# One decoder layer in float32: packed query, key and router products, routing by match-and-replace, and another order and grain of work and weight loads around the first experts

## What is computed

```
xn   = rms_norm(h, g);  proj = xn @ w_in          # columns: cq 384, ckv 256, kr 32, rx 1024, rg 1024, gates 2048
q    = rms_norm(cq) @ w_uq                        # 8 heads x (64 plain + 32 rotary)
kv   = rms_norm(ckv) @ w_ukv                      # 8 heads x (64 key + 64 value); rotary key kr is shared by the heads
attn = softmax(q k^T * scale, causal) @ v @ w_ao
rec  = RG-LRU(conv(rx), gates) * gelu(rg) @ w_ro
h    = h + (sigmoid(ga) * attn + sigmoid(gr) * rec) @ w_out
x2   = rms_norm(h);  logits = x2 @ w_router + b_router       # 32 experts
top 4 of 32, gates = softmax of the four logits
h    = h + sum over the chosen experts of gate * (swiglu(x2 @ w_up[e] + b_up[e]) @ w_down[e] + b_down[e])
out  = rms_norm(h)[16:]
```

## Time and profile before

| | |
|---|---|
| median of 3 executions | 1181.56 us (1181.07 to 1181.73) |
| the profiled execution | 1181.36 us |
| its span, first to last instruction | 1179.6 us |
| TensorE busy | 1141.4 us, 97% |
| VectorE, ScalarE busy | 228.5 us (19%), 187.3 us (16%) |
| chain that ended last | PE 73%, DMA 25%, ACT 1% |
| moved | 442.03 MB, mean 375 GB/s |
| TensorE clock granted | full in all 40 slices of the page, mean 0.999 |

### The profile page before, as it was taken

The page is one execution under the profiler, slowest core; times in us unless marked ns, Lnnn a source line. Parts: engine busy times, 40 slices in busy tenths (PEclk is TensorE's granted clock), DMA queues, the critical chain, the costliest instruction groups (busy, mean ns, idle before and its releaser), DMA issues.

```text
span 1179.6 us, 13314 instructions
## 1 busy us (share of the span) xinstructions
PE 1141.4 (97%) x5598; PEld 530.4 (45%) x5598; DVE 228.5 (19%) x528; ACT 187.3 (16%) x404; POOL 0.2 (0%) x4
## 2 busy tenths in 40 slices
PE   9999999999999999999999999999998989898997
PEld 7767888855243333333343433333333333333332
DVE  4555621114111111111111112111111111111112
ACT  2257620002011110101010111101000001010102
POOL 0000000000000000000000000000000000000000
PEclk9999999999999999999999999999999999999999
DMA  9834434387999999999999999999999999999996
GB/s 377 348 143 179 150 119 162 146 344 290 399 422 429 428 431 432 432 431 430 434 430 432 432 432 431 430 434 430 432 432 432 431 431 433 431 431 432 426 426 272
DMA packets 26128, 442.03 MB, mean 375 GB/s; under 512 B 4144, under 2 KB 4656, under 8 KB 7408
## 3 DMA queue, kind: packets, MB, share of 16 engines
q1 hardware_dynamic: 23472, 439.19, 88.3%
q10 hardware_dynamic: 2624, 2.39, 0.6%
HBM read 440.52 MB, written 1.05 MB: 374 GB/s over the span
## 4 chain that ended last, share of the span: by engine, by line
PE 73%; DMA 25%; ACT 1%; DVE 0%; issue 0%; SPq 0%; another core or an unknown queue 0%; ACTq 0%; DVEq 0%
PE ps L880 28%; DMA work<-in_w_exp_dram 24%; PE ps L899 12%; PE ps L538 11%; PE ps L867 4%; PE ps L855 4%; PE ps L747 2%; PE ps L810 2%; PE ps L830 2%; PE ps L771 1%; PE ps L615 1%; ACT work L1297 1%; PE ps L889 1%; DMA ring<-in_w_mix_dram 1%; PE ps L581 1%; PE ps L861 1%
## 5 line engine op out<-in xcount | busy, mean ns | idle before, releaser
L880 PE MATMUL ps<-ring,work 128*64 128x512 f32 x1536 | 341.0, 595 | 12.6 <-DMA ring<-in_w_exp_dram 12.6
L880 PEld LDWEIGHTS ps<-ring,work 128*64 128x64 f32 x1536 | 109.0, 137 | 228.9 <-issue 217.6
L1733 DVE TENSOR_SCALAR work<-ps 128x512 f32<-128x512 f32 x32 | 22.1, 691 | 742.2 <-PE ps L880 742.2
L538 PE MATMUL ps<-work,ring 128*128 128x256 f32 (+2 forms) x576 | 129.5, 384 | 0.0
L880 PE MATMUL ps<-work 128*64 128x512 f32 x512 | 116.2, 596 | 5.1 <-DMA work<-in_w_exp_dram 5.1
L899 PE MATMUL ps<-ring,work 128*64 128x512 f32 x512 | 113.6, 595 | 5.5 <-ACT work L1297 3.8
L899 PE MATMUL ps<-work 128*64 128x512 f32 x512 | 114.0, 596 | 3.9 <-ACT work L1297 3.8
L538 PEld LDWEIGHTS ps<-work,ring 128*128 128x128 f32 (+1 forms) x576 | 107.1, 188 | 19.1 <-issue 1.2
L880 PEld LDWEIGHTS ps<-work 128*64 128x64 f32 x512 | 34.9, 137 | 82.1 <-issue 72.6
L899 PEld LDWEIGHTS ps<-ring,work 128*64 128x64 f32 x512 | 35.5, 137 | 73.4 <-issue 65.4
L899 PEld LDWEIGHTS ps<-work 128*64 128x64 f32 x512 | 35.2, 137 | 72.8 <-issue 62.8
(11 more groups left out here) (237 smaller groups left out, 617.3 us busy)
## 6 DMA issues: line engine op xcount, KB each, us to landing
ring<-in_w_exp_dram SPq DMA_DIRECT2D x52, 4096.0 KB, 39.9
work<-in_w_exp_dram SPq DMA_DIRECT2D x26, 4096.0 KB, 39.9
ring<-in_w_exp_dram SPq DMA_DIRECT2D x23, 2048.0 KB, 10.8
ring<-in_w_mix_dram SPq DMA_DIRECT2D x29, 1024.0 KB, 7.1
work<-in_w_exp_dram SPq DMA_DIRECT2D x10, 2048.0 KB, 12.2
work<-in_w_exp_dram SPq DMA_DIRECT2D x4, 1024.0 KB, 44.4
...
```

Source lines behind the costliest of these rows:

```text
L538: ins = nc.tensor.matmul(ps[part:part + width, b, 0:hi - lo], wv[:, k, o:o + width], xnT[:, k, lo:hi], start=(k == 0), stop=(k == KT - 1))
L880: ins = nc.tensor.matmul(ps[CAP * c:CAP * c + CAP, b, :], xeT[:, k, CAP * (u % 2):CAP * (u % 2) + CAP], wu[:, k % SPAN, 512 * q:512 * q + ...
L1733: V.tensor_scalar(hg, ps[:, 0, :], LIMIT, None, ALU.min).then_inc(glu_ready, 1)
```

## The change

The 32-column product of the rotary key is done in four column groups, whose partial sums a second small product adds up (`fold`) beside the rotation. The query weights are repacked on the host so that six full tiles of 128 columns replace eight of 96: four with two heads' plain parts each, two with four heads' rotary parts; the query rotation is one set of four 32x32 matmuls in one bank, and VectorE's part works on 128 partitions. The router has its weights as stationary operand in four column groups and h^T moving; ScalarE copies the result and a small product turns and adds it (`fold(i)`). The mask comes from match-and-replace: the first four columns of `lgs` hold a large constant, so that MAX8 gives that and the top four, match-and-replace writes a constant over these, and a comparison with the logits gives `selm`, per tile (`choose`). Seeds, bias and router are put in another order; the norm of tile 1 is made in halves; of expert 0's gathers the second goes behind k = 1, the b_down product behind `up`; expert 1 has its own order with the scatters behind `up` and the gathers between the steps of `down`; `down` frees slot by slot. SP loads five units (`HALVED`) of experts 2 and 3 in halves and uses units of 2 MB until expert 7, pairs from expert 8 on. Constants for rotation, cos and sin are spread over all 128 partitions, which makes the constants 32 columns (16 KB) longer.

The diff, cut to its core and less indented (`...` marks what is left out):

```diff
+HALVED = (0, 4, 5, 10, 11)
...
-    spe.wait_ge(xn2_ready, TT)
+    spe.wait_ge(xn2_ready, TT + 1)
     fetch(1, 4)
...
+    for n in range(2, 8):
+        for c in range(UNITS_E):
+            r = UNITS_E * (n % 2) + c
+            used = M0 + PER_EXPERT * (n - 2) + SPAN * c
+            if n < 4 and r in HALVED:
+                for h in range(SPAN):
+                    spe.wait_ge(weights_used, used + h + 1)
+                    spe.dma_start(RING[r][:, SLOT * h:SLOT * h + SLOT],
+                                  w_exp[n, c // 2, :, UNIT * (c % 2) + SLOT * h:UNIT * (c % 2) + SLOT * h + SLOT])\
+                       .then_inc(unit_loaded[r], 16)
+            else:
+                spe.wait_ge(weights_used, used + SPAN)
+                fetch(n, c)
...
-        spe.dma_start(PAIR[3 * (u % 2) + p], w_exp[it * UNROLL + (u + 4), p, :, :])\
+        spe.dma_start(PAIR[3 * (u % 2) + p], w_exp[it * UNROLL + (u + 8), p, :, :])\
...
-    project(("kr", 0), OFF_KR, ROPE, 0, T, part=NOPE, last=True)
...
+    for k in range(KT):
+        q = ROPE * (k % 4)
+        ins = nc.tensor.matmul(ps[q:q + ROPE, b, 0:T], wv[:, k, o:o + ROPE], xnT[:, k, :], start=(k < 4), stop=(k >= 4))
+        if k == 0:
+            settle(ins)
+    ins.then_inc(proj_done, 1)
...
-    nc.tensor.matmul(ps[NOPE:QD, 6, 0:T], rotm, kh[NOPE:QD, 0, :], start=True, stop=True).then_inc(krot_done, 1)
+    nc.tensor.matmul(ps[NOPE:QD, 6, 0:T], rotm, krope, start=True, stop=True)
+    nc.tensor.matmul(ps[NOPE:QD, 7, 0:T], foldm, krope, start=True, stop=True).then_inc(krot_done, 1)
...
-    for h in range(HEADS):
-        n = load_at[("uq", 384 * (h // 4))]
+    for t in range(6):
...
-            ins = nc.tensor.matmul(ps[0:QD, b, 0:SEQ], wv[:, k, QD * (h % 4):QD * (h % 4) + QD], cq[:, k, :],
+            ins = nc.tensor.matmul(ps[:, b, 0:SEQ], wv[:, k, P * (t % 3):P * (t % 3) + P], cq[:, k, :],
...
-        if g >= 2:
-            if g == 2:
-                pe.wait_ge(proj_read, JOB[("q", HEADS - 1)] + 1)
-                pe.wait_ge(rope_ready, 1)
-                pe.wait_ge(lora_var, 2)
-            for r in (2 * g - 4, 2 * g - 3):
-                nc.tensor.matmul(ps[NOPE:QD, 4 + r, :].rearrange("p (h t) -> p h t", h=2), rotm,
-                                 qh[NOPE:QD, 2 * r:2 * r + 2, :], start=True, stop=True).then_inc(qrot_done, 1)
+        if g == 2:
+            pe.wait_ge(proj_read, JOB[("q", 5)] + 1)
+            pe.wait_ge(lora_var, 2)
+            for j in range(4):
+                ins = nc.tensor.matmul(ps[ROPE * j:ROPE * j + ROPE, 4, :].rearrange("p (k t) -> p k t", k=2),
+                                       rotm[ROPE * j:ROPE * j + ROPE, :], qrope[ROPE * j:ROPE * j + ROPE, :, :],
+                                       start=True, stop=True)
+            ins.then_inc(qrot_done, 1)
...
-            ins = nc.tensor.matmul(ps[:, i, 0:E], hT[:, k, :], wr[:, k, :], start=(k == 0), stop=(k == KT - 1))
-        ins.then_inc(logits_done, 1)
+            q = E * (k % 4)
+            ins = nc.tensor.matmul(ps[q:q + E, 0, 0:P], wr[:, k, :], hT[:, k, :], start=(k < 4), stop=(k >= 4))
+        ins.then_inc(logT_done, 1)
+    def fold(i):
+        pe.wait_ge(logT_ready, i + 1)
+        nc.tensor.matmul(ps[:, 1, E * i:E * i + E], logT, pick_e[:, 0:E], start=True, stop=True).then_inc(logits_done, 1)
...
     pe.wait_ge(wr_ready, 1)
     router(0)
-    turn_h(1)
-    router(1)
+    turn_h(1, 0)
+    fold(0)
+    turn_h(1, 1)
...
-    pe.wait_ge(sel0_ready, 1)
-    pe.wait_ge(logits_read, 1)
-    up_bias(0)
+    router(1)
     seed(0, 1)
+    fold(1)
+    seed(1, 0)
     pe.wait_ge(mask_ready, 1)
     nc.tensor.matmul(ps[:, 2, 0:E], upper, selm[:, 0, :], start=True, stop=True)
     nc.tensor.matmul(ps[:, 2, E:2 * E], ones, selm[:, 0, :], start=True, stop=False, skip_group_check=True)
+    pe.wait_ge(mask_ready, 2)
     nc.tensor.matmul(ps[:, 2, E:2 * E], upper, selm[:, 1, :], start=False, stop=True, skip_group_check=True)\
       .then_inc(pos_done, 1)
     nc.tensor.matmul(ps[:, 3, 0:E], ones, selm[:, 0, :], start=True, stop=False)
     nc.tensor.matmul(ps[:, 3, 0:E], ones, selm[:, 1, :], start=False, stop=True).then_inc(pos_done, 1)
...
+    up_bias(0)
...
-    seed(1, 0)
     pe.wait_ge(xn2_ready, TT)
     pe.wait_ge(pick_ready, 2)
     pe.wait_ge(counts_read, 1)
-    gather(0).then_inc(gather_done, 1)
-    gather(1).then_inc(gather_done, 1)
+    gather(0, 3).then_inc(gather_done, 1)
     seed(1, 1).then_inc(seeded, 1)
...
     def first_between(k):
+        if k == 1:
+            pe.wait_ge(xn2_ready, TT + 1)
+            gather(1, 2).then_inc(gather_done, 1)
         if k == 4:
             pe.wait_ge(gate_ready, 1)
...
-        if k == 6:
-            pe.wait_ge(y_ready, 1)
-            pe.wait_ge(bdn_in, 32)
-            for i in range(TT):
-                for c in range(2):
-                    nc.tensor.matmul(ps[:, 4 + 2 * i + c, :], gpickT[CAP * c:CAP * c + E, i, :], y[CAP * c:CAP * c + E, :],
-                                     start=False, stop=True, skip_group_check=True)
-    up(0, alone(0, 1), first_start, first_between)
+    up(0, alone(0), first_start, first_between)
+    pe.wait_ge(y_ready, 1)
+    pe.wait_ge(bdn_in, 32)
+    for i in range(TT):
+        for c in range(2):
+            nc.tensor.matmul(ps[:, 4 + 2 * i + c, :], gpickT[CAP * c:CAP * c + E, i, :], y[CAP * c:CAP * c + E, :],
+                             start=False, stop=True, skip_group_check=True)
     pe.wait_ge(route_ready, 1)
...
+    second = alone(1)
+    up(1, second, lambda k: None, lambda k: None)
+    pe.wait_ge(y_ready, 2)
+    pe.wait_ge(gpickT_ready, 1)
+    scatter(0, y, gpickT)
+    scatter(1, y, gpickT)
+    pe.wait_ge(route_ready, 2)
+    turn_route(2).then_inc(gpickT_done, 1)
+    pe.wait_ge(hidden_read, 2)
+    up_bias(0)
+    pe.wait_ge(gpickT_ready, 2)
+    pe.wait_ge(act_ready, 2)
+    turn_act()
+    for t in range(4):
+        if t < 2:
+            pe.wait_ge(actT_ready, 3 + t)
+        if t % SPAN == 0:
+            wd = second(4 + t // SPAN)
+        down_step(wd[:, SLOT * (t % 2):SLOT * (t % 2) + SLOT], t, actT, 3).then_inc(weights_used, 1)
+        if t == 1:
+            pe.wait_ge(pick_ready, 4)
+            gather(0, 2).then_inc(gather_done, 1)
+        if t == 2:
+            pe.wait_ge(xeT_ready, 3)
+            gather(1, 2).then_inc(gather_done, 1)
+    for n in range(2, 8, 2):
+        even(n, alone(n))
+        odd(n + 1, alone(n + 1))
+    with pe.Fori(0, PAIRED) as it:
         for u in range(UNROLL):
-            n = it * UNROLL + (u + 4)
+            n = it * UNROLL + (u + 8)
             if u % 2 == 0:
...
                 act.wait_ge(conv_ready, i - 1)
             ins = nc.scalar.activation(rxp[:, i % 2, CONV - 1:], ps[:, b, 0:T], ACT.Copy)
         elif kind == "q":
-            ins = nc.scalar.activation(qh[0:QD, i, :], ps[0:QD, b, 0:SEQ], ACT.Copy)
+            if i % 3 == 2:
+                ins = nc.scalar.activation(qrope[:, i // 3, :], ps[:, b, 0:SEQ], ACT.Copy)
+            else:
+                h = 4 * (i // 3) + 2 * (i % 3)
+                nc.scalar.activation(qh[0:NOPE, h, :], ps[0:NOPE, b, 0:SEQ], ACT.Copy)
...
+    act.wait_ge(h_half, 2)
+    nc.scalar.activation(sqx[:, 0, :], X[:, 0, :], ACT.Square, accum_out=ss2[:, 0:1]).then_inc(h_sumsq, 1)
+    read_hT(0)
+    act.wait_ge(h_var, 1)
+    nc.scalar.activation(rs2[:, 0:1], ss2[:, 0:1], ACT.Sqrt).then_inc(h_std, 1)
+    read_logT(0)
+    act.wait_ge(h_half, 3)
+    nc.scalar.activation(sqx[:, 1, 0:512], X[:, 1, 0:512], ACT.Square, accum_out=ss2[:, 1:2]).then_inc(h_sumsq, 1)
+    read_hT(1)
+    act.wait_ge(h_half, 4)
+    nc.scalar.activation(sqx[:, 1, 512:1024], X[:, 1, 512:1024], ACT.Square, accum_out=ss2h).then_inc(h_sumsq, 1)
+    act.wait_ge(h_sumsq, 3)
+    act.wait_ge(h_var, 2)
+    nc.scalar.activation(rs2[:, 1:2], ss2h, ACT.Sqrt, bias=ssb, scale=1.0 / D).then_inc(h_std, 1)
+    read_logT(1)
+    act.wait_ge(mask_ready, TT)
     for i in range(TT):
...
-        read_gather(h)
+    act.wait_ge(gather_done, 1)
+    read_gather(0, 3)
     act.wait_ge(seeded, 1)
-    act.wait_ge(xn2_ready, TT)
+    act.wait_ge(xn2_ready, TT + 1)
     act.wait_ge(hT_done, 2 * TT)
     for c in range(2):
         act.dma_start(y[CAP * c:CAP * c + E, :], b_down[0, :, 512 * c:512 * c + 512]).then_inc(bdn_in, 16)
+    act.wait_ge(gather_done, 2)
+    read_gather(1, 2)
...
+    link(V.tensor_tensor(kh[NOPE:QD, 0, :], ps[NOPE:QD, 7, 0:T], cosT, ALU.mult))
...
-    sin2 = ca[NOPE:QD, CA["sin"][0] + N_META:CA["sin"][1]].rearrange("p (a t) -> p a t", a=1).broadcast_to([ROPE, 2, SEQ])
-    for g in range(4):
-        dve.wait_ge(qrot_done, g + 1)
-        q2 = qh[NOPE:QD, 2 * g:2 * g + 2, :]
-        V.tensor_tensor(ropeu[NOPE:QD, :, :], ps[NOPE:QD, 4 + g, :].rearrange("p (h t) -> p h t", h=2), sin2, ALU.mult)
-        link(V.tensor_tensor(q2, q2, cos2, ALU.mult))
-        ins = V.tensor_tensor(q2, q2, ropeu[NOPE:QD, :, :], ALU.add)
-        if g < 3:
-            ins.then_inc(rope_ready, 1)
```

(49 more changed lines are left out.)

182 lines of the change are left out of this document (94 added, 88 removed).

## The result

The changed kernel takes **1170.57 us** (median of 4 runs, 1170.37 to 1170.99) against 1181.48 us (1181.07 to 1181.73) for the kernel before beside it: ratio 0.9908, interval 0.9896 to 0.9921. 1170.0 was predicted, and the range of 1167 to 1175 holds the result. The profiled execution spans 1168.7 us (before: 1179.6), 10.9 less.

The account below looks back on a forecast made before the run. The weight stream, started by expert 0's first slot release, was taken to bound the kernel, with TensorE filling the mixer before it. 7.5 + 3.4 + 1.0 - 0.5 = 11.4 us off 1181.36 gave 1170.0, range 1167 to 1175.

Parts of the forecast that it names:

- What bounds it: Whole kernel: end set by one stream of 30 experts' weights, 874 us, starting when expert 0 frees its first slot.
- Part 1: Mixer: packed key, queries and rotation save TensorE time, all on the path, 7.5 us; bounds 2.1 to 7.8.
- The rule that spoke against the rotation: Query rotation: row tiles can't share a PSUM bank simultaneously, which would make the saving 2.65 us less; forecast went against it.
- rival (a): Mixer: packed products don't overlap (key, rotation or both), 2.7 to 5.3 us missing, 1172.7 to 1175.3; chance 0.11.
- Part 2: Routing: expert 0 starts 11.0 us after the output projection's end, 3.4 us earlier; bounds 2.1 to 4.2.
- Part 3: Weight stream: gaps of 4.0 us (1.5 + 2.2 + 0.3) instead of 5, 1.0 gained; smaller pieces lose 0.5.
- I take 0.5: Weight stream: 24 smaller units run at a slightly lower rate, 0.5 us lost; bounds 0 to 2.9.
- a fixed tail, which the change doesn't touch: Kernel's end: the rest of the span behind the last weights, from 1158 to 1179.6 together with the stream's gaps, unchanged.
- The hole in the stream: Weight stream's start, sign: DMA near full at 287 to 300 us except one hole of 2 us.
- Rival (c): Routing to expert 0: clock falls to half through expert 0, 19 us lost against 11.4 gained, 1189; chance 0.03.
- Rival (b): Mixer: saving swallowed by ScalarE or VectorE, which set the first LRU pass, leaving 1177.5; chance 0.07.
- (d): Kernel's end: nothing changes, as the stream is limited elsewhere, 1181.4; chance 0.01.

Follow-up runs that it names:

- experiment 1: Kernel before with the packed key, query and rotation products alone: 1172.49 us (before 1181.32), ratio 0.9925.
- experiment 7: Kernel before with 32 unused columns added to the constants, nothing else: 1180.0 us (before 1181.41), ratio 0.9990.
- 9: Kernel before with only the constants' SBUF buffer 32 columns wider, moving the buffers behind it: 1179.69 us (before 1181.40), ratio 0.9984.
- 2: Changed kernel with the old weight stream (only expert 2's unit 0 in halves, pairs from expert 4 on): 1169.22 us.
- 3: Changed kernel with its half units kept, but pairs of units from expert 4 on instead of 8: 1168.59 us.
- 5: Changed kernel with pairs of units from expert 4 on and expert 2's unit 1 also in halves: 1169.31 us.
- 8: Changed kernel with DRAM constants as short as before, the fold's columns loaded apart, SBUF buffer still wide: 1170.20 us, ratio to before 0.9904.
- experiment 6: Changed kernel with two gate products of the mixer made twice: 1176.71 us, ratio to before 0.9960.
- experiment 10: Changed kernel with VectorE's rank computation made 18 more times, so TensorE stands still before expert 0: 1177.30 us.

## Why the prediction was right

**What bounds it: right.** The end follows the first release: where it came 6.31 us later by mixer work, the first store came 6.28 later and the time rose by 6.1; where it came 6.13 later by standing still, 6.18 and 6.7; 7.1 us of work in expert 4 cost nothing. The absolute sum was less complete than it looked. 1158 and 5 us of gaps give 1163, but the last weights land at 1168.3 (the landing that starts at 1127.35, 40.93 us long), so 5 us of the stream stood in no term. Both kernels have them, and the difference doesn't need them.

**Part 1, 7.5 us: right, less the start.** The key and the rotation overlap, the six full tiles of queries take three quarters of the time of eight, and experiment 1 shows 7.23 + 0.28 = 7.5. (The terms' own upper bounds add up to 7.6, not 7.8.) The working had no term for the start: the first product on weights came at 10.48 instead of 9.86, so 6.9 arrived. Over the other kernels run that start lies between 9.88 and 10.63, in six of the nine kernels with the whole change above 10.4, and at 9.95 in experiment 7. So the length of the constants alone is not it; what sets it stays open. The rule that spoke against the rotation did not hold here: the eight records (four products) in four row tiles and one bank took 0.99 us, all begun within 0.4 us, as long as the bias row's 1.02 in two banks. That rule (the Trainium skill, TensorEngine Tiling (Array Packing), Restrictions and Gotchas) would have cost 2.65 us, and rival (a) with it is gone.

**Part 2, 3.4 us: right.** Expert 0 starts 10.67 us behind the projection instead of the 11.0 forecast, the release is at 12.58 instead of 12.8, the down product at 31.35 against 31.3. Match-and-replace takes 0.08 + 0.18 us, where 0.3 was taken between bounds of 0.2 and 1.6. The mask is ready at 5.9 and not at 6.5. Only 0.1 of this is VectorE's, 1.2 us from logits to mask instead of 1.3; the rest came before, as the second router ended at 3.5 and not at 4.0. The pick, ready at 7.2 and not at 7.9, is not on the path: the gather starts at 7.8, when TensorE's own bias row ends. The gather took 1.98 us instead of 1.8, which gives some of it back.

**Part 3: the sum was right and its terms were not.** At the start the gaps came as worked out: 5.1 - 4.3 = 0.8 us, near the 1.0 taken, and the first 16 us lack 3.6, near the 1.5 + 2.2. But the 0.8 does not arrive. With the buffers moved, the old stream takes 888.8 to 889.2 us from release to store (experiments 7, 9 and 1) and the new one 889.46. "I take 0.5" for the smaller pieces was too little: the whole units of experts 4 to 7 cost 1.0 to 2.0. Its bounds of 0 to 2.9 held, but they looked at the rate alone, and in the profiled executions the cost lies in the store behind the last expert, where the working had said "a fixed tail, which the change doesn't touch". On the other side a gain of 1.4 to 1.7 us was missing, the 58.15 us instead of 58.27 for two late experts from buffers that lie 128 bytes further on. The constants' growth had been costed at 0.04 us of transfer. That these errors cancel was luck, and 1170.0 is closer than its terms deserve. In medians: packing and place -8.8 (experiment 1), routing and order -3.3 (2), half units -0.6 (3), whole units for experts 4 to 7 +2.0, sum -10.7; as each is the difference to the one before, they add up by construction.

**The range.** Its low end was added up wrongly: 3.6 us below 1170.0 is 1166.4, and the good ends of the parts (0.8, 1.5 and 0.5) give 1167.2. Nothing hangs on it here.

**Signs.** The key, the rotation and expert 0's start came out as listed, and the projection's end is 0.6 us later than listed, by the later start. The late period is 58.15 and not 58.27 us. The hole in the stream is there, but the list had it between 287 and 300 us, against its own sum (19.1 to 21.4 us behind 260.1, so 279 to 281.5), and it lies between 280 and 283. From the first product on, no wait of TensorE on the DMA is on the chain before the landing that starts at 796 us, and the rate between 339 and 589 us is 431 GB/s. One "wrong" sign appeared without being one: the granted clock fell before the tail.

```profile
1000.91 8.78 PE L920 MATMUL ps<-ring,work 128*64 128x512 f32 x32 [1.98 <-DMA ring<-in_w_exp_dram]
```

```profile
1000.00:1002.00 2.00, 1.09 (x6) 0.57 (x8) 0.00 (x0) 0.00 (x0) 0.00 (x0) 1.00 0.99 426
1002.00:1004.00 2.00, 2.00 (x7) 0.66 (x5) 0.00 (x0) 0.00 (x0) 0.00 (x0) 0.54 0.99 426
1004.00:1006.00 2.00, 2.00 (x8) 0.73 (x6) 0.00 (x0) 0.00 (x0) 0.00 (x0) 0.60 1.07 459
```

TensorE had waited 1.98 us for a landing, and its clock was then at half for most of 4 us, while the stream went on at 426 GB/s on average between 1000 and 1010 us. Experiments 3, 5 and 8, with a mean granted clock of 0.994, take 889.3 to 889.6 us from release to store, and experiment 6, with 0.999, takes 889.4: where the stream sets the end, such falls cost nothing. Rival (c) had the mechanism, and experiment 10 its price at the place where it would count: some 1.9 us, not 19. Rival (b) is excluded by experiment 1, whose time fell by more than its projection's end moved, and (d) by the measured time and experiment 6.
